# The sample states of an HGRN2 layer: outer products taken from the tensor engine and given to DMA, ScalarE and VectorE

## The reference, cut to what matters

```python
q = silu(q_raw) * 128 ** -0.5
f = lb + (1 - lb) * sigmoid(f_raw)          # q, f, k = 1 - f: (sample, head, 128)
S_new = f[..., :, None] * S_old + k[..., :, None] * v[..., None, :]
o = einsum('d,dv->v', q, S_new)             # for each sample and head; S_new is an output too
```

## Time and profile before

| what | value |
|---|---|
| median of 3 runs | 1168.5 us (1167.05 to 1168.92) |
| the profiled execution's own time | 1167.45 us |
| its span, from first to last instruction | 1165.6 us |
| busy PE / DVE / ACT / POOL | 1154.3 / 1001.4 / 567.7 / 69.4 us |
| share of PE, DVE, ACT in the span | 99%, 86%, 49% |
| DMA, mean | 204 GB/s |

### The profile page before, as it was taken

One profiled execution on the slowest core, in us unless ns is written; L12 is line 12 of the kernel. 1 busy time (PEld: TensorE's weight loads), 2 busy tenths in 40 slices (PEclk: granted clock), 3 DMA queues, 4 the chain that ended last, 5 costly groups with the idle time before them and its releaser, 6 DMA issues.

```text
span 1165.6 us, 30910 instructions
## 1 busy us (share of the span) xinstructions
PE 1154.3 (99%) x12445; PEld 1035.0 (89%) x12445; DVE 1001.4 (86%) x1564; ACT 567.7 (49%) x821; POOL 69.4 (6%) x104
## 2 busy tenths in 40 slices
PE   8999999999999999999999999999999999999997
PEld 7888888888888899899998999989989999999886
DVE  6788799778867898998989989888899999998577
ACT  6545645654545744444444444444444444444544
POOL 2122310100000200000000000000000000000031
PEclk9999999999999999999999999999999999999999
DMA  7767876766566566666666666666666666667595
GB/s 254 233 206 208 237 208 198 233 193 190 181 212 198 177 217 194 197 193 213 209 196 194 196 213 206 200 192 195 216 194 205 211 206 199 200 212 227 178 230 150
DMA packets 198825, 238.07 MB, mean 204 GB/s; under 512 B 12682, under 2 KB 158449, under 8 KB 198480
## 3 DMA queue, kind: packets, MB, share of 16 engines
q1 hardware_dynamic: 192528, 222.13, 61.0%
q0 software_dynamic: 4864, 13.99, 4.2%
q10 hardware_dynamic: 1360, 0.92, 0.3%
HBM read 228.46 MB, written 9.01 MB: 204 GB/s over the span
## 4 chain that ended last, share of the span: by engine, by line
PE 92%; DVE 4%; DMA 2%; ACT 1%; issue 1%; SPq 0%; DVEq 0%; ACTq 0%
PE acc L2355 13%; PE acc L1957 10%; PE acc L1959 10%; PE acc L1961 10%; PE acc L2396 7%; PE acc L2358 6%; PE acc L2357 6%; PE acc L2336 6%; PE acc L2338 6%; PE wrk L2336 4%; PE wrk L2338 4%; PE acc L2399 2%; PE acc L2398 2%; DVE hl L997 2%; PE wrk L2114 1%; DMA raw<-in_w_in_dram 1%
## 5 line engine op out<-in xcount | busy, mean ns | idle before, releaser
L997 DVE SCALAR_TENSOR_TENSOR hl<-raw,hl 128x1024 f16<-128x1024 f32 x414 | 493.7, 1220 | 56.3 <-ACT hl L628 53.6
L628 ACT ACTIVATE hl<-raw 128x1024 f16<-128x1024 f32 x414 | 420.3, 1051 | 166.4 <-DMA raw<-in_w_down_dram 88.5
L2355 PE MATMUL acc<-nrm,hl 128*128 128x264 f16 x1344 | 274.8, 276 | 0.3 <-DVE tg L1501 0.3
L1959 PE MATMUL acc<-nrm,hl 128*128 128x264 f16 x920 | 253.9, 276 | 0.0
L1961 PE MATMUL acc<-nrm,hl 128*128 128x264 f16 x920 | 253.9, 276 | 0.0
L1957 PE MATMUL acc<-nrm,hl 128*128 128x264 f16 x920 | 253.9, 276 | 0.0
L2357 PE MATMUL acc<-nrm,hl 128*128 128x264 f16 x672 | 185.5, 276 | 0.0
L2358 PE MATMUL acc<-nrm,hl 128*128 128x264 f16 x672 | 185.5, 276 | 0.0
L2355 PEld LDWEIGHTS acc<-nrm,hl 128*128 128x128 f16 x1344 | 129.0, 98 | 18.1 <-DVE tg L1501 0.6
L2396 PE MATMUL acc<-big,hl 128*128 128x264 f16 x704 | 130.2, 276 | 0.0
L1957 PEld LDWEIGHTS acc<-nrm,hl 128*128 128x128 f16 x920 | 90.2, 98 | 13.3 <-issue 0.3
(11 more groups left out here) (493 smaller groups left out, 2246.6 us busy)
## 6 DMA issues: line engine op xcount, KB each, us to landing
raw<-in_w_gate_up_dram SPq DMA_DIRECT2D x168, 512.0 KB, 4.5
raw<-in_w_down_dram SPq DMA_DIRECT2D x88, 512.0 KB, 4.2
raw<-in_w_in_dram SPq DMA_DIRECT2D x80, 512.0 KB, 4.5
raw<-in_w_out_dram SPq DMA_DIRECT2D x32, 512.0 KB, 5.0
raw<-in_w_ple_gate_dram SPq DMA_DIRECT2D x32, 512.0 KB, 5.4
state<-in_state_hgrn_dram POOLq DMA_DIRECT2D x8, 512.0 KB, 7.3
out_new_hgrn_sample_dram<-state POOLq DMA_DIRECT2D x8, 512.0 KB, 5.4
raw<-in_w_gate_up_dram SPq DMA_DIRECT2D x16, 256.0 KB, 3.4
```

What stands on the lines that cost most here:

```text
L628: nc.scalar.activation(hi[:, st.hl_slot(j, half), :], raw[:, st.raw_slot(j), :], ACT.Copy, scale=WSCALE).then_inc(hi_done, 1)
L997: stt(lo[:, st.hl_slot(j, half), :], raw[:, st.raw_slot(j), :], WSCALE, hi[:, st.hl_slot(j, half), :], ALU.mult, ALU.subtract).then_inc(lo ...
L1959: mm(out, wh, x_lo[:, kt, :], start=False, stop=False)
L2355: mm(out, wh, n_hi[:, kt, :], start=jj == 0 and kk == 0, stop=False, skip_group_check=bool(up))
```

## The change

Old state and product now come together without TensorE. VectorE copies the values of four heads into one tile (`vs_pack`), TensorE transposes it once (job `vs_0` on turn 26, `vs_1` on 51), ScalarE copies the 32 rows out, and GpSimd's queue writes them to memory (16 KB) and, once they have landed, reads the rows of one head back to all 128 partitions (`rows_to_all`, 512 KB, one of two buffers `v_bc`). ScalarE scales both factors in place, four blocks of 128x128 a time: old state by f (`state_kept`), the value rows by k (`kv_ready`), 8 parts for a pair, on the turns `PART_AT`. VectorE adds the two in one instruction of 128x1024 per head (`new_states`). The high half of a state is made on the turns `S_HI_AT`, the low half on the turn after, and the `os` job is on the turns `S_OUT_AT` = 42, 50, 64, 72, where it was on 36, 48, 60, 68. The sums over the samples' outputs move from turn 71 to 74, their root from 72 to 75, their mixing from 75 to 77. Loads and stores on GpSimd's queue change places, and its memsets of the wide tiles go.

```diff
-SAMPLE_AT = (26, 38, 50, 58)
-BUF_AT, U_LAST_AT, OSS_AT = 44, (73, 81), 71
-RMS_AT, ROOT_AT, SAMPLE_ROOT_AT = 64, 65, 72
-O_NORM_AT, O_MIX_AT, SAMPLE_MIX_AT = (66, 67, 69, 71), (68, 70, 72, 74), 75
+PART_AT = ((28, 29, 30, 31, 32, 33, 34, 35), (40, 41, 42, 43, 44, 44, 45, 46),
+           (52, 53, 54, 55, 56, 57, 58, 59), (60, 64, 64, 65, 66, 67, 68, 68))
+ADD_AT = tuple((at[3] + 1, at[7] + 1) for at in PART_AT)
+S_HI_AT = ((36, 40), (46, 48), (59, 62), (67, 70))
+S_OUT_AT = (42, 50, 64, 72)
+ROWS_AT = (26, 51)
+BUF_AT, U_LAST_AT, OSS_AT = 44, (73, 81), 74
+RMS_AT, ROOT_AT, SAMPLE_ROOT_AT = 64, 65, 75
+O_NORM_AT, O_MIX_AT, SAMPLE_MIX_AT = (66, 67, 69, 71), (68, 70, 72, 74), 77
-X_FIRST = 27
+X_ROWS, X_FIRST, X_LAST = 16, 24, 28
...
+            x_blocks(range(BUF_BEHIND, X_ROWS))
+            rows_written(0)
+            x_blocks(range(X_ROWS, X_ROWS + 2))
+            pool.wait_ge(vs_out, 16)
+            rows_to_all(0)
+            rows_to_all(1)
+            x_blocks(range(X_ROWS + 2, X_FIRST))
             for p in range(PAIRS):
+                if p == 2:
+                    rows_written(1)
+                    pool.wait_ge(vs_out, 32)
+                    rows_to_all(4)
+                    rows_to_all(5)
                 for h in (2 * p, 2 * p + 1):
-                    pool.wait_ge(drained["dve"], drain_of(f"ou_{p}_3")[1])
+                    pool.wait_ge(state_new, h + 1)
                     pool.dma_start(io["new_hgrn_sample"][0, :, h, :, :].rearrange("b d v -> d b v"),
                                    state[:, h % 2, :, :]).then_inc(state_out[h % 2], 16)
+                    if p % 2 == 0:
+                        rows_to_all(h + 2)
+                    if h == 0:
+                        x_blocks(range(X_FIRST, X_LAST))
                 if p == 0:
-                    x_blocks(range(X_FIRST, 4 * (SEQ // 32)))
+                    x_blocks(range(X_LAST, 4 * (SEQ // 32)))
...
+            def sample_part(p, n):
+                old, h = n % 4 // 2 == p % 2, 2 * p + n // 4
+                x, gains = (state[:, h % 2], f_all) if old else (v_bc[h % 2], k_all)
+                if old:
+                    act.wait_ge(state_in[h % 2], 16 * (p + 1))
+                    act.wait_ge(acc_free, TPG * (3 * (p // 2) + 3))
+                else:
+                    act.wait_ge(v_bc_in[h % 2], 16 * (p + 1))
+                for b in range(4 * (n % 2), 4 * (n % 2) + 4):
+                    last = nc.scalar.activation(x[:, b, :], x[:, b, :], ACT.Copy, scale=gains[:, h, SEQ + b:SEQ + b + 1])
+                if n % 2:
+                    last.then_inc(state_kept if old else kv_ready, 1)
+
+            def state_high(h):
+                act.wait_ge(state_new, h + 1)
...
-            def pair_states(p, bs):
...
+            def new_states(h):
+                dve.wait_ge(state_kept, h + 1)
+                dve.wait_ge(kv_ready, h + 1)
+                tt(state[:, h % 2], state[:, h % 2], v_bc[h % 2], ALU.add).then_inc(state_new, 1)
...
+            def sample_rest(p, b):
+                if b in ADD_AT[p]:
+                    new_states(2 * p + ADD_AT[p].index(b))
+                if b - 1 in S_HI_AT[p]:
+                    h = 2 * p + S_HI_AT[p].index(b - 1)
                     dve.wait_ge(s_hi_ready, h + 1)
                     tt(s_lo[h % 2], state[:, h % 2], s_hi[h % 2], ALU.subtract).then_inc(s_lo_ready, 1)
-                elif r == 10:
+                if b == S_OUT_AT[p]:
                     wait_job(f"os_{p}")
...
-            def sample_kv(p):
...
-            def outer(p, bs):
...
+            def sample_values(c):
+                pe.wait_ge(vs_packed, c + 1)
+                out = job(f"vs_{c}")
+                nc.tensor.transpose(out[0:4 * NSAMP, 0:P], vs_pack, ident[:]).then_inc(job_done, 1)
+                yield
...
+            def sample_jobs(p, b):
+                if b == S_OUT_AT[p]:
                     out = job(f"os_{p}")
                     pe.wait_ge(q16_ready, p // 2 + 1)
                     pe.wait_ge(s_lo_ready, 2 * p + 2)
```

More of the change, by code:

```diff
@@ L199 @@
             JOBS += [(f"sf_{_c}", "act")]
[L200 to L207, removed]
+    if _b in ROWS_AT:
+        JOBS += [(f"vs_{ROWS_AT.index(_b)}", "act")]
+    if _b in S_OUT_AT:
+        JOBS += [(f"os_{S_OUT_AT.index(_b)}", "dve")]
     if _b == BUF_AT:
@@ L308, in build @@
         sc16 = xe[:, 4160:5696].bitcast(F16).rearrange("p (n a h t) -> p n a h t", n=2, a=3, h=4)
-        kv_smp = xe[:, 0:512].bitcast(F16).rearrange("p (s h j d) -> p s h j d", s=2, h=2, j=2)
+        vs_tok, vs_pack = xe[0:4 * NSAMP, 0:P], xe[:, P:P + 4 * NSAMP]
+        v_bc = [xe[:, n:n + 1024].rearrange("p (b v) -> p b v", b=NSAMP) for n in (3136, 2048)]
+        v_rows = nc.dram_tensor("v_rows", (QUADS, 4 * NSAMP, P), F32, kind="Internal").ap()
         buf_tok = xe[0:NSAMP * POOL_BUF, 1024:2048]
@@ L568, in _ @@
             pool.wait_ge(drained["dve"], drain_of(f"n1_{KT - 1}")[1])
[L569 to L573, removed]
+            nc.gpsimd.memset(scores[:, 0:2], 0.0).then_inc(zero_ready, 1)
             pool.wait_ge(masks_ready, 1)
@@ L602, in _ @@
                 if p == 1:
-                    pool.wait_ge(job_done, job_value("sb"))
-                    nc.gpsimd.memset(kv_wide[1], 0.0).then_inc(zero_ready, 1)
                     pool.dma_start(io["new_pool_sample"][0, :, 0:POOL_BUF - 1, :], io["state_pool"][0, :, 1:POOL_BUF, :])\
                         .then_inc(buf_stored, 16)
+            for n in range(2):
+                last = nc.gpsimd.memset(win[n][:, :, 0:WPAD], 0.0)
+            last.then_inc(zero_ready, 1)
             pool.wait_ge(drained["act"], drain_of("ut_1")[1])
@@ L778, in quad_part, with value_rows @@
                         .then_inc(sf_out, 16)
[L780 to L794, removed]
+            def value_rows(c):
+                wait_job(f"vs_{c}")
+                nc.scalar.activation(vs_tok, wrk[0:4 * NSAMP, JOB[f"vs_{c}"] % JOB_BANKS, 0:P], ACT.Copy)\
+                    .then_inc(drained["act"], 1)
+            def sample_part(p, n):
[12 more added lines that the diff above has]
+                act.wait_ge(state_new, h + 1)
+                if h > 1:
+                    wait_job(f"os_{h // 2 - 1}")
+                nc.scalar.activation(s_hi[h % 2], state[:, h % 2], ACT.Copy).then_inc(s_hi_ready, 1)
             def mix_high(j):
@@ L828, in _ @@
                     quad_part(c, b - QUAD_AT[c])
+                if b in ROWS_AT:
+                    value_rows(ROWS_AT.index(b))
                 for p in range(PAIRS):
-                    sample_part(p, b - SAMPLE_AT[p])
+                    for n in range(8):
+                        if PART_AT[p][n] == b:
+                            sample_part(p, n)
+                    if b in S_HI_AT[p]:
+                        state_high(2 * p + S_HI_AT[p].index(b))
                 if b in U_LAST_AT:
@@ L1195, in level_total @@
                 tt(f[:, :, :, 0, 0], f[:, :, :, 0, 0], f[:, :, :, 1, 0], ALU.mult).then_inc(tot_ready, 1)
-            def pair_states(p, bs):
[L1199 to L1209, removed]
+            def new_states(h):
+                dve.wait_ge(state_kept, h + 1)
+                dve.wait_ge(kv_ready, h + 1)
+                tt(state[:, h % 2], state[:, h % 2], v_bc[h % 2], ALU.add).then_inc(state_new, 1)
             def sample_halves(c):
-                hs, wide = slice(4 * c, 4 * c + 4), kv_wide[c]
+                hs = slice(4 * c, 4 * c + 4)
                 dve.wait_ge(acc_free, TPG * (3 * c + 3))
-                dve.wait_ge(zero_ready, c + 1)
+                nc.vector.tensor_copy(vs_pack.rearrange("p (h b) -> p h b", h=4), v_all[:, hs, SEQ:TOK]).then_inc(vs_packed, 1)
                 q_s = q_all[:, hs, SEQ:TOK]
@@ L1218, in sample_halves @@
                 stt(q16[:, hs, :, 1], q_s, Q_UP, q16[:, hs, :, 0], ALU.mult, ALU.subtract).then_inc(q16_ready, 1)
[L1219 to L1224, removed]
             def take_diagonal(c):
@@ L1313, in window @@
                 wait_job(f"ut_{g // 2}")
+                dve.wait_ge(zero_ready, 2)
                 dst = win[0]
@@ L2254, in in_jobs @@
                     yield from quad_jobs(c, b - QUAD_AT[c])
+                if b in ROWS_AT:
+                    yield from sample_values(ROWS_AT.index(b))
                 for p in range(PAIRS):
-                    yield from sample_jobs(p, b - SAMPLE_AT[p])
+                    yield from sample_jobs(p, b)
                 if b == BUF_AT:
```

29 lines of the change are left out of this document (12 added, 17 removed).

## The result

The changed kernel takes **1181.3 us** (median of 6 runs, 1179.8 to 1183.2), the one before 1168.4 in the same comparison (6 runs, 1167.1 to 1170.1): ratio 1.0109, interval 1.0099 to 1.0119. It is slower, as forecast, but by 12.9 us where the sum said 7.3, and 0.3 us above the range. The profiled execution took 1182.1 us with a span of 1180.3, which is 14.7 over the span of before; the mean granted clock went from 0.997 to 0.991.

The account below looks back on a forecast made before the run. TensorE, working 99% of the span, was taken as the bound. Saved work -5.1 plus waits 1.7, 4.7, 2.85 and 3.15 gave +7.3 us, a median of 1175.8 us, range 1169 to 1181.

Parts of the forecast that it names:

- the range: Forecast of the changed kernel's median time: eight in ten between 1169 and 1181 us; all high bounds given as 1180.5.
- Saved work, -5.1: On TensorE: transposes and outer products go, two fp32 transposes come; net -5.1 us, bounds -5.3 and -4.8.
- The four waits: TensorE waits for VectorE's low half on turns 42, 50, 64, 72: 1.7, 4.7, 2.85 and 3.15 us.
- The anchor on turn 50: Turn 50's wait reckoned from TensorE's end of block 47: low half ready 12.55 us later, TensorE there at 7.8.
- Rivals 1 and 2: 1: halves ready in time, no waits, 1163.4 us, chance 0.11. 2: no wait on turn 50 only, 1171.1, chance 0.13.
- ScalarE at 1.0 a part: Four 128x128 scalings on ScalarE take 1.0 us, hidden beside other work; cost 0, bounds -0.3 and +1.3.
- Rows in time: Value rows through memory land before ScalarE needs them on turns 30 and 54; cost 0, bound +3 for the second round.
- rival 3: Second round of rows lands late, so the tiles of turn 55 come late: +3 us, 1178.8, chance 0.10.
- The clock priced at 0: The sum held no term for TensorE's clock falling to half behind the new waits; only a rival did.
- Rival 4: After turn 50's wait TensorE runs a stretch at 1.2 GHz, losing 1.7 us: 1177.5, chance 0.08.

Follow-up runs that it names:

- e1_fill: Changed kernel with 16, 42, 25 and 29 matmuls on constant weights put ahead of the waits of turns 42, 50, 64, 72; 1176.2 us.
- e11_kept_early: e7_spread_rows with VectorE making the fourth pair's old-state products (turns 63, 65), some parts and a high half earlier, last low half behind the mixing; 1165.5 us.
- e4_before_near: Kernel before, only each output job two turns earlier, one turn behind the second low half; 1189.7 us, ratio 1.0183.
- e5_low_first: Changed kernel with the low half ahead of VectorE's split on turns 41, 49, 63 and 71; 1174.5 us, ratio 1.0054.
- e7_spread_rows: Changed kernel with jobs on turns 44, 52, 64, 72, last two pairs' second halves a turn earlier, parts needing no rows first; 1170.3 us.
- e3_later: Changed kernel with the first three pairs' output jobs two turns later (44, 52, 66), the last left at 72; 1177.6 us, ratio 1.0086.
- e2_fill_last: Changed kernel with 29 matmuls put ahead of the last wait (turn 72) alone; 1178.8 us, ratio 1.0096.

## Why the prediction was right in part and wrong in size

- **Saved work, -5.1: right.** It is not read off one row (the outer products and transposes leave 0.44 us a time, as on turn 28, whose block went from 3.58 to 3.14), but the account closes with it: after (15.0 against 14.7), e1_fill (9.1 against 8.9 in the blocks) and, less well, e11_kept_early (1167.3 - 5.1 + 0.5 + 2.1 = 1164.8 against 1165.5).
- **The four waits: right.** Forecast 1.7, 4.7, 2.85, 3.15; measured 1.9, 4.9, 2.9, 3.3, each within its bounds, released by the named instruction. e4_before_near and e5_low_first show that the cause is the one turn of distance and the split in it. The anchor on turn 50 held: the low half was to be ready 12.55 us after block 47, which ended at 173.37, and it ended at 185.87.
- **Rivals 1 and 2** (no waits; none on turn 50) did not come. VectorE is 5.5 us lighter in all (the prediction said 9), and that moved none of its starts on turns 41, 63 and 71: its split begins 0.2, 1.2 and 1.6 us behind the first main matmul of the next block, before and after alike.
- **ScalarE at 1.0 a part: too low, without effect.** Four scalings last 1.26 us, 1.17 to the next instruction: by the earlier trace rows a 128x128 without a vector operand was 0.31 long, these are 0.39. In after it stayed covered, so 0 was right there. In e7_spread_rows, with TensorE's slack gone, the cover was thin and it became the wait of turn 68. The Trainium skill (ScalarE: Activation LUTs, What ACT_TABLE_LOAD costs) gives 280 ns and 0.833 for each element where one operand is a vector of the partitions, with 93 ns of overlap to the next: 0.387 and 0.29 by an estimate from it. The trace agrees, 0.387 median and 1.17 for four.
- **Rows in time: right for after, by a cover that the prediction did not name.** Landing is 7.6 us in the median of eight, not 4.5. The second round took 9.2 us from the copy (forecast 9.5 to 12.5) and ScalarE waited 0.7 us for rows in all. But that rests on the wait of turn 50: without it, in e3_later, rival 3 came at its +3 (3.1 us).
- **The clock priced at 0: the step that failed.** The sum had "-5.1 + 1.7 + 4.7 + 2.85 + 3.15" with no term for it. Rival 4 had a price of 1.7 for the right event, but behind turn 50 alone and with a chance of 0.08. It came behind all four waits in that execution, for 17.1 us in place of 3.4, and cost 6.8 us by the spans, 7.5 to 7.8 by the blocks. What misled was to treat the fall as a rare accident of the longest wait. The earlier trace rows showed the half clock already in the start-up, behind waits of 1.1 us and less, and from 17 us to the end of the sample work on turn 74 TensorE in before has no idle stretch over 0.2 us from which "no fall" could have been read. The Trainium skill (TensorE: Matmul & The Clock Gate, What's actually happening) puts the throttled clock as the default that activity lifts. The trace agrees behind every wait of 2.9 us or more.
- **The range: its upper end was added up too low.** The upper bounds of the terms with the late rows are -4.8 + 2.0 + 6.0 + 3.1 + 3.4 + 3.0 = 12.7, which is 1181.2 and not 1180.5, still with nothing for the clock. That the measured 1181.3 lies so near it says nothing for the mechanism: neither ScalarE's parts nor late rows cost TensorE anything in after, and the clock did.

## What to carry to other kernels

Where TensorE is the bound, its waits of 2.9 us and longer cost here their own length and another 1.4 to 2.9 us for the half clock behind them, and those of some 2 us did so now and then; write that term beside every forecast wait. A job that waits for VectorE's work of the turn before pays VectorE's whole queue of that turn, so ask at which place of its queue the producer stands, not only in which turn. And a transfer that looks covered may be covered by the very wait that one means to remove.

## What the runs showed of the hardware

The waits of TensorE at which it loses 0.5 us or more, on turns 34 to 73, over the profiled executions of all kernels, and the granted clock around their end:

| Lost at the wait | Cases | Half clock at its end |
| --- | --- | --- |
| 0.5 to 1.3 us | 11 | none |
| 1.9 to 2.3 us | 8 | 2 (after, turn 42; e5_low_first, turn 72), 3.41 us each |
| 2.9 to 4.9 us | 17 | 17: eight times 3.41 us, nine times 6.83 us |

(Two waits of 2.1 us that were followed by another of 3.4 within a microsecond are not counted.) Length does not decide alone: e2_fill_last runs the same instructions as after up to turn 71, and its wait of 1.9 us on turn 42 had no half clock behind it, while the 4.9 us of turn 50 had 6.83 us in place of 3.41. The start of the half clock is not tied to the end of the wait either, from 1.3 us behind it (e4_before_near, turn 34) to 2.1 ahead of it (e2_fill_last, turn 50). Where the blocks can be compared with those of another run, 3.41 us of half clock cost 1.4 to 1.8 us, and 6.83 us cost 1.9 to 2.9. What decides between 3.41 and 6.83 stays open. In the six runs of after the mean clock varies too, between 0.989 and 0.993, and the times go with it (1183.2 us at 0.989, 1179.8 at 0.993), so much of their spread may be this; only one of them has a trace.

Filling a wait with useless products of TensorE is worth the clock: 112 products of 128x264 into a bank that is overwritten anyway gave 5.1 us in the medians and 6.5 in the blocks, where 1.2 of a possible 7.8 went to another wait.
